# Side work of a ten-stage transformer kernel: three adaLN items and four folds go from stage 0 into Mamba, the gate pieces go later, and FFN second blocks get two products of a weight slot with itself

## The reference, cut to what matters

```python
m = c_act @ w + b
shift, scale, gate = jnp.split(m, 3, axis=-1)
h = rmsnorm(x, g) * (1.0 + scale[:, None, :]) + shift[:, None, :]
x = x + 0.5 * g * swiglu(h, ffn_w_gate[i, 0], ffn_w_up[i, 0], ffn_w_down[i, 0])
```

## Time and profile before

| | |
|---|---|
| runs | 1854.56, 1856.36, 1871.04 us; median 1856.36 |
| the profiled execution | 1855.45 us, span 1853.7 us, mean granted TensorE clock 0.982 |
| TensorE busy | 1765.2 us, 95% of the span |
| VectorE busy | 1440.4 us, 78% |
| ScalarE busy | 962.2 us, 52% |
| loaded from memory | 423.74 MB, 230 GB/s over the span |

### The profile page before, as it was taken

How to read it: one execution, slowest core, us unless ns; L and a number is a source line. 1 busy time by engine, 2 the same in 40 slices (tenths; PEclk the granted TensorE clock), 3 DMA queues, 4 the chain that set the end, 5 groups by cost and what they waited for, 6 DMA issues and landing times.

```text
span 1853.7 us, 34027 instructions
## 1 busy us (share of the span) xinstructions
PE 1765.2 (95%) x14590; PEld 1711.8 (92%) x14590; DVE 1440.4 (78%) x1714; ACT 962.2 (52%) x1257; POOL 0.2 (0%) x4
## 2 busy tenths in 40 slices
PE   5999999999999999999989999898999999989999
PEld 4999999998899999998979999897999988979999
DVE  7799988887799879986558998655888867457666
ACT  4434466666443453436564445556555555665553
POOL 0000000000000000000000000000000000000000
PEclk8999999999999999999999999999999998999999
DMA  9999834433698859883436987232487543325551
GB/s 396 417 376 370 325 114 160 160 137 137 225 387 350 322 213 406 334 324 132 164 114 263 379 356 286 113 135 102 171 291 250 195 164 136 132 71 182 181 190 37
DMA packets 68149, 426.23 MB, mean 230 GB/s; under 512 B 7488, under 2 KB 10832, under 8 KB 31824
## 3 DMA queue, kind: packets, MB, share of 16 engines
q1 hardware_dynamic: 63936, 416.22, 58.9%
q10 hardware_dynamic: 4112, 8.62, 1.4%
HBM read 423.74 MB, written 3.17 MB: 230 GB/s over the span
## 4 chain that ended last, share of the span: by engine, by line
PE 91%; DVE 3%; ACT 3%; DMA 2%; issue 1%; ACTq 0%; DVEq 0%; SPq 0%
PE bank L1447 26%; PE bank L1449 26%; PE bank L1448 26%; DMA mix<-mods 2%; PE bank L1513 2%; PE bank L1460 2%; PE bank L1462 1%; PE bank L1780 1%; PE bank L1467 1%; DVE w_lo L866 1%; PE bank L1622 1%; PE bank L1761 1%; PE bank L1657 0%; PE bank L1781 0%; PE bank L1714 0%
## 5 line engine op out<-in xcount | busy, mean ns | idle before, releaser
L1447 PE MATMUL bank<-h_hi,w_hi 128*128 128x256 f32 x2864 | 802.2, 280 | 4.2 <-DVE w_lo L866 3.6
L1449 PE MATMUL bank<-h_hi,w_lo 128*128 128x256 f32 x2864 | 796.9, 278 | 0.0
L1448 PE MATMUL bank<-h_lo,w_hi 128*128 128x256 f32 x2864 | 796.8, 278 | 0.0
L866 DVE TENSOR_TENSOR w_lo<-raw,w_hi 128x2048 fp32r<-128x2048 f32 x276 | 630.5, 2285 | 117.3 <-ACT w_hi L466 116.6
L466 ACT ACTIVATE w_hi<-raw 128x2048 fp32r<-128x2048 f32 x276 | 527.7, 1912 | 146.7 <-PE bank L1449 134.6
L1447 PEld LDWEIGHTS bank<-h_hi,w_hi 128*128 128x128 f32 x2864 | 540.2, 189 | 8.0 <-DVE w_lo L866 4.0
L1449 PEld LDWEIGHTS bank<-h_hi,w_lo 128*128 128x128 f32 x2864 | 542.1, 189 | 0.0
L1448 PEld LDWEIGHTS bank<-h_lo,w_hi 128*128 128x128 f32 x2864 | 539.3, 188 | 0.1
L1447 PE MATMUL bank<-a_hi,w_hi 128*128 128x256 f32 x1280 | 358.4, 280 | 2.1 <-DVE w_lo L866 2.1
L1448 PE MATMUL bank<-a_lo,w_hi 128*128 128x256 f32 x1280 | 355.5, 278 | 0.0
L1449 PE MATMUL bank<-a_hi,w_lo 128*128 128x256 f32 x1280 | 355.4, 278 | 0.0
(11 more groups left out here) (259 smaller groups left out, 1660.4 us busy)
## 6 DMA issues: line engine op xcount, KB each, us to landing
raw<-weights SPq DMA_DIRECT2D x276, 1024.0 KB, 4.9
modws<-mods SPq DMA_DIRECT2D x144, 768.0 KB, 6.9
mix<-mods SPq DMA_DIRECT2D x5, 1024.0 KB, 8.8
mix<-mods ACTq DMA_DIRECT2D x8, 512.0 KB, 12.8
biases<-scratch ACTq DMA_DIRECT2D x1, 2048.0 KB, 13.8
mix<-biases ACTq DMA_DIRECT2D x4, 512.0 KB, 3.8
modws<-mods SPq DMA_DIRECT2D x1, 1024.0 KB, 11.7
x<-xin SPq DMA_DIRECT2D x1, 1024.0 KB, 10.9
```

Of the source, the lines that this page charges most:

```text
L866: eng.tensor_tensor(w_lo[g % NW][:, :], raw[g % NRAW][:, :], w_hi[g % NW][:, :], ALU.subtract).then_inc(sems["wlo"], 1)
L1447: eng.matmul(dst, ah, bh, start=start, stop=False, skip_group_check=skip)
L1448: eng.matmul(dst, ah, bl, start=False, stop=False, skip_group_check=skip)
L1449: return eng.matmul(dst, al, bh, start=False, stop=stop, skip_group_check=skip)
```

## The change

Items 29, 30, 31 and the four folds of job 2 leave stage 0 and are put in front of the first w_lo of Mamba's bodies 1 to 7, one in each. The folds of job 2 use `modw` slots 0 and 1 as scratch instead of `turned`, since `mix` is Mamba's. The loads of items 32 to 35 wait for these folds and are issued at Mamba's last block. In stage 0's list gate pieces 4 to 7 and the two gate folds stand behind 14 items of job 1 instead of 8, and the list starts two slots later. In the second block of each FFN and convolutional FFN stage TensorE computes, ahead of each half, one product of the block's w_hi slot with itself into bank 6, which nobody reads.

```diff
+SIDE_FROM = {0: 2}
+MAMBA_SIDE = [None] + [("item", q) for q in (29, 30, 31)] + [("fold", (2, part)) for part in range(4)]
+HELD = range(32, 36)
...
     if st == 0:
-        out = ([("gate", n) for n in range(4)] + out[:8] + [("gate", n) for n in range(4, 8)]
-               + [("gate_fold", 0), ("gate_fold", 1)] + out[8:])
-    return out
+        out = ([("gate", n) for n in range(4)] + out[:14] + [("gate", n) for n in range(4, 8)]
+               + [("gate_fold", 0), ("gate_fold", 1)] + out[14:])
+    return [w for w in out if w not in MAMBA_SIDE]
...
+        skip = SIDE_FROM.get(st, 0)
         for w in work:
-            table.setdefault((st, *SIDE_STEPS[SIDE_SLOTS * at // total]), []).append(w)
+            table.setdefault((st, *SIDE_STEPS[skip + (SIDE_SLOTS - skip) * at // total]), []).append(w)
...
+                    if q in HELD and q % 4 < 2:
+                        k.wait("fold", 2, b=2 + q % 4)
...
-                            load_mod(q + 4)
+                            if q + 4 not in HELD:
+                                load_mod(q + 4)
+                    if kind == "mamba" and b == NBLK[kind] - 1:
+                        for q in HELD:
+                            load_mod(q)
...
-                flat = turned[half]
+                flat = modw[half] if j == 2 else turned[half]
...
+                def side(i):
+                    if MAMBA_SIDE[i]:
+                        kind, what = MAMBA_SIDE[i]
+                        item(what) if kind == "item" else fold(*what)
+
                 def body(i, a, b):
                     more = i > 0
+                    side(i)
                     split(st, i, a, b)
...
+                        if pulse:
+                            eng.matmul(bank[6][:, 0:T], hi[:, 0, 0:P], hi[:, 0, :], start=True, stop=True)
...
-                    gemm(bank[5], st, i, a, b)
+                    gemm(bank[5], st, i, a, b, pulse=first)
```

More of the change, by code:

```diff
@@ L1449, in three, with gemm @@
                 return eng.matmul(dst, al, bh, start=False, stop=stop, skip_group_check=skip)
-            def gemm(dst, st, i=0, a=0, b=0, tokens=False, first=False, between=None):
+            def gemm(dst, st, i=0, a=0, b=0, tokens=False, first=False, between=None, pulse=False):
                 hi, lo = [w.rearrange("p (k n) -> p k n", k=KT) for w in begin(st, i, a, b)]
```

## The result

The changed kernel takes 1838.39 us (median of 20 runs, 1830.49 to 1849.77) against 1855.24 us for the kernel before (20 runs, 1840.77 to 1871.04). The ratio is 0.9918, with a 95% interval of 0.9899 to 0.9936. All ratios here are of fast runs alone, which leaves out one run of e14, 1870.97 us. The forecast was 1848.5 with a range from 1843: the time lies 10.1 us under the forecast and 4.6 us under the range. The profiled execution took 1839.61 us.

A forecast was written before the change was run, and what follows sets the result against it. TensorE was taken to bound the kernel, with stage 0 losing 8.16 us to VectorE's late w_lo. 1855.45 - 8.16 - 0.45 + 1.36 = 1848.20, forecast 1848.5 us, range about 1843 to 1856.

The forecast's parts named there:

- What bounds the kernel: TensorE, busy 95% of the span; stage 0 loses 8.16 us before block 12 to VectorE's late w_lo, all coming back.
- the end of the stage: Stage 0's end: TensorE's 0.37 us idle before the gate fold's product goes; 0.45 us taken, bounds 0 and 0.65.
- a sum of 8.38: Stage 0's predicted gain: 8.16 for the stops plus 0.45 at the end, less 0.23 for its two products.
- item 9's load: Stage 0's DMA queue: walked to arrive at 106.4, with VectorE waiting there some 1.5 us.
- block 14 as the least margin: Stage 0: w_lo done at 110.4, wanted by TensorE at 112.66; 2.3 us, the least margin after that point.
- The DMA rate: Stage 0's loads walked at 417.5 GB/s; at about 358 block 14 would be 5.0 us late, the sum 1853.2.
- Mamba: Moved steps ahead of the first w_lo of bodies 1 to 7 cost zero; 0.9 us to spare in body 1.
- The product's price: Twelve extra matmuls in second blocks of six FFN and conv-FFN stages cost 1.36 us; bounds nothing and 2.7.
- The sum: Whole kernel: 1855.45 - 8.16 - 0.45 + 1.36 = 1848.20 us, with matmuls at 0.113 us each.
- That the products keep the clock up: Rival at later stage entries: full clock at all seven slow ones, 1848.2 - 9.8 = 1838.4; clock rival's chance 0.06.
- The bound on entries: Later stage entries with low clock, 1.4 us each, may change by two either way, 2.8 us.
- the stop's loss at half clock: Stage 0: part of the 8.16 us ran at 1.2 GHz after the second stop, 3.24 us, and comes back too.

The follow-up runs named there:

- e14: The changed kernel without its twelve products, all moves of side work kept; 1847.97 us, ratio 0.9951 to the kernel before.
- e13: The changed kernel itself, unedited, timed again on one chip beside its version without products; 1840.3 us, ratio 0.9898 to the kernel before.
- e2: The kernel before with only the twelve products added, side work where it was; 1853.09 us, ratio 0.9976 to the kernel before.
- e5: The kernel before, old side-work list, with two bf16 products of constants in the second block of the five later stages; 1842.08 us, ratio 0.9951.
- e12: The changed kernel with one bf16 product in each of the five later stages and one fp32 product in stage 0 instead; 1835.97 us, ratio 0.9853.
- e6: The changed kernel with bf16 products in later stages, items and folds back in stage 0, gate pieces still late; 1842.24 us, ratio 0.9943.
- e7: The changed kernel with half-width fp32 products of constants in the later stages instead, none in stage 0; 1836.4 us, ratio 0.9905.

## Why the prediction was wrong

- **What bounds the kernel** held. The stretch from 80 to 110 and the end of the stage gave 8.41 us for a sum of 8.38, with both queues walked right: item 9's load, its wait, block 14 as the least margin later on.
- **The DMA rate.** The sum took 417.5 GB/s from the rows, and the rows after show 417, 413 and 415 in the same stretch, with item 9's load 0.3 us from its walked time. The Trainium skill's limit of about 358 GB/s for loads from HBM ("DMA: Bandwidth & Descriptors", section "Bandwidth") would have put block 14 five microseconds late. It was 2.0 us early; the measurement decides. The same section of the Trainium skill gives about 358 as each core's share when both cores of an HBM domain stream, and 425 GB/s as measured with one core alone; this kernel runs on one core.
- **Mamba** held: zero, with 0.9 us to spare in body 1 as worked out.
- **The product's price is the step that failed.** "I price them like their neighbours, 12 x 0.113 = 1.36 us", with "below, nothing" as the bound. Their own cost was even smaller: the second block takes 5.60 us instead of 5.44, so 0.16 for two and 0.96 for twelve. But they also act on what follows: with them the median falls, by 7.7 us from e14 to e13 and by about 4.5 in e2, and three stages that had entered at the longer pace left it right behind a product, where none of 19 without one did. Bounding from below by nothing excluded a gain without a reason that excludes it.
- **The sum rested on one pace.** 0.113 us a matmul was read in stage 0 and in no other stage. The same profile had stages 7 and 9 at 0.118 with the clock at 1.00 (the first fence of pace above), and the runs shown spread from 1854.56 to 1871.04, 16 us, which no term explained. Reading one such stretch per stage would have shown a term of 6.5 us a stage that differs from run to run, and the question of what sets it.
- **The rivals.** "That the products keep the clock up" named 1838.4 and the median came at 1838.39, but by another way: e13 and e14 have the same mean clock, 0.982, and are 7.7 us apart. A number met by a wrong mechanism is no support for it. The bound on entries, two either way, was also too tight for a single trace: the pair of profiles differs in four, some 5.6 us, and in 3.5 us of clock inside stage 8, for which the sum had no term.
- **A stop and the clock.** The sum had part of the stop's loss at half clock. e2 shows such a fall after a shorter one: it stops 2.41 us before 94.19, and then

```profile
94.19:98.19 4.00, 4.00 (x24) 4.00 (x25) 0.62 (x1) 0.00 (x0) 0.00 (x0) 0.68 1.03 423
```

  In the kernel before the stop of 2.10 us was followed by no fall and that of 3.24 us by one; e5's 2.14 us was followed by a clock of 0.58 over the next 4 us. The Trainium skill ("TensorE: Matmul & The Clock Gate", section "Why this matters for your kernels") asks for no gaps above about 3 us; e2's 2.41 us and e5's 2.14 us already cost clock.

What the runs account for, from before to the changed kernel on one chip (e13's): 15.9 us between the medians; 8.2 with the moves alone (e14), 7.7 more with the products. As the products cost 1.0 themselves, the pace would have to give 8.7, which is 1.3 of the five later stages at the shorter pace (6.5 each). The traces' own count gives less, two stages net in twenty or half a stage per run, some 3.3 us and 2.3 net of the cost; four traces are few, and what the odds are stays open, as does stage 0, which drew the longer pace in four of the ten traces without a product there, in one of six with an fp32r product, and in e12 with an fp32 one.

## What to carry to other kernels

Read the spacing of matmuls in every stage, not in one, before a sum uses it: where a long stream runs at two paces under the same clock, the spread of the runs is a term of its own, and a change of 1% can be nothing but its odds. A product that nobody reads is priced by its neighbours only for itself; what it does to the stream behind it needs a run. Moving VectorE's side work into a stage that has gaps for it is sound, and two queues walked with durations from rows gave it within 0.1 us in the trace; what remains in the crowded stage must still be done by its end, as e6's median shows.

## What the runs showed of the hardware

- A stream of 128x256 fp32r matmuls runs at 113 or 118 ns a matmul over 25 blocks at granted clock 1.00, 136.00 against 141.33 us. What in the engine differs is not shown.
- Without another product and without a long interval it keeps the pace of its first block (15 of 15 stages). An interval of 0.2 to 0.4 us in the stream can turn it either way (stage 4 of e7, stage 0 of four traces).
- Of the stages that entered at 118 ns, a bf16 product brought 113 in 11 of 11, at 0.10 to 0.15 us each; a product of the slot with itself in three of nine. No rule by type follows: in Mamba all 119 blocks right behind the heads' fp32 products ran at 118.
- The product of a slot with itself adds 0.08 us to the stream, less than its neighbours' 0.113, and the fp32 product of e7, half as wide, 0.46 (second block 6.36 us).
- A stop of TensorE of 2.10 us was followed by full clock, stops of 2.14 (e5), 2.41 (e2) and 3.24 us by a fall.
